# A hybrid gMLP and mLSTM decoder layer on 8 cores: the up projection moved between the head tiles, w_down kept in SBUF, the mLSTM gates computed as rows

## The reference

```python
def _layer(...):
    a = rmsnorm(h, norm_mix)
    z = a @ w_in                                     # (B, T, 3080)
    u, vg, q, k, vm, o, zi, zf = jnp.split(z, SPLITS, axis=-1)
    u = gelu(u); vg = layernorm(gelu(vg), gm_ln_g, gm_ln_b)
    y_gm = _gmlp_mix(u, vg, gm_ws, gm_bs, gm_len)    # u * (tril(W_s) v + b), per chunk
    ig = zi + ml_b_i; lf = log_sigmoid(zf + ml_b_f)
    hm, state = _mlstm(q, k, vm, ig, lf, state, ml_len)
    y_ml = sigmoid(o) * rmsnorm(hm per head)
    h = h + concat([y_gm, y_ml]) @ w_out
    f = rmsnorm(h, norm_ffn) @ w_up                  # 1024 -> 4096
    h = h + square(relu(f)) @ w_down                 # 4096 -> 1024
    gate = sigmoid(rmsnorm(h, norm_ple) @ w_ple_gate)
    return h + gate * (pe @ w_ple_proj), state, vg   # then a final rmsnorm

def _mlstm_chunk(carry, inp):                        # 128 prompt tokens, or 8 of a sample
    b = cumsum(lf); g = b + m
    D = b_t - b_s + ig_s                             # masked to s <= t
    m_t = maximum(g, max_s D)
    w_intra = exp(D - m_t); w_inter = exp(g - m_t)
    s = (q k^T) * w_intra
    num = s v + w_inter * (q C); den = sum(s) + w_inter * (q n)
    h = num / maximum(abs(den), exp(-m_t))
    w_end = exp(D_last - m_last); dec = exp(g_last - m_last)
    C = dec * C + (w_end k)^T v; n = dec * n + sum(w_end k)
```

## Time and profile before

| what | us |
|---|---|
| three runs | 1131.55, 1148.24, 1186.08 |
| profiled execution | 1132.5 |
| its span on the slowest core | 1130.0 |
| spans of the eight cores | 1104.7 to 1130.0 |
| granted TensorE clock of the cores, mean | 0.931 to 0.941 |
| busy PE / DVE / ACT / POOL | 943.0 / 574.1 / 464.0 / 339.5 |

### The profile page before, as it was taken

One profiled execution on the slowest core, in us unless ns is written; L12 is line 12 of the kernel. 1 busy time (PEld: TensorE's weight loads), 2 busy tenths in 40 slices (PEclk: granted clock), 3 DMA queues, 4 the chain that ended last, 5 costly groups with the idle time before them and its releaser, 6 DMA issues.

```text
span 1129.9 us, 17655 instructions; the slowest of 8 cores (1104.7 to 1130.0 us)
## 1 busy us (share of the span) xinstructions
PE 943.0 (83%) x5508; PEld 499.0 (44%) x5508; DVE 574.1 (51%) x1424; ACT 464.0 (41%) x992; POOL 339.5 (30%) x519
## 2 busy tenths in 40 slices
PE   0179877798889978597879998999899999999965
PEld 0034444444444444254435553555355445547622
DVE  0126677658787687774203641563066227416513
ACT  0227656585655755244303531442153224305312
POOL 4125553535454554432200221212111212112100
PEclk9989887898989989789989998999999999999997
DMA  9996001522111101999999369937972993399381
GB/s 167 191 156 85 14 35 57 93 39 76 39 38 57 57 17 41 181 169 137 207 167 142 89 137 202 143 107 157 169 146 85 171 183 109 93 169 176 81 137 48
DMA packets 109149, 128.98 MB, mean 114 GB/s; under 512 B 14594, under 2 KB 91522, under 8 KB 109058
## 3 DMA queue, kind: packets, MB, share of 16 engines
q0 software_dynamic: 74416, 72.96, 45.0%
q1 hardware_dynamic: 34642, 54.90, 16.0%
HBM read 177.97 MB, written 22.84 MB: 178 GB/s over the span
## 4 chain that ended last, share of the span: by engine, by line
PE 65%; DMA 17%; DVE 7%; issue 5%; ACT 2%; SPq 2%; POOL 1%; another core or an unknown queue 0%; DVEq 0%; POOLq 0%; ACTq 0%
PE pb L192 62%; DMA AR<-w_down 11%; DVE AR L454 4%; PE pb L199 3%; DMA AR<-snT 3%; DVE AR L464 2%; ACT AR L434 2%; SPq L341 2%; DMA AR<-hscr 2%; DMA AR<-sC 1%; POOL AR L454 1%; DVE AR L471 0%; DMA AR<-xp 0%; ACT L434 0%
## 5 line engine op out<-in xcount | busy, mean ns | idle before, releaser
L192 PE MATMUL pb<-AR 128*128 128x512 bf16 (+4 forms) x4786 | 901.0, 347 | 97.6 <-DMA AR<-w_down 32.4
L192 PEld LDWEIGHTS pb<-AR 128*128 128x128 bf16 x4786 | 451.4, 102 | 514.9 <-issue 166.9
L434 ACT ACTIVATE AR<-pb 128x384 f32<-128x384 f32 (+4 forms) x379 | 192.7, 523 | 325.6 <-PE pb L192 211.9
L434 ACT ACTIVATE AR<-AR 128x128 f32<-128x128 f32 (+2 forms) x357 | 189.6, 554 | 244.2 <-DVE AR L454 117.5
L454 DVE TENSOR_TENSOR AR<-AR 128x4 f32<-128x4 f32 (+5 forms) x521 | 194.7, 391 | 178.0 <-ACT AR L434 153.4
L454 POOL TENSOR_TENSOR AR<-AR 128x1 f32<-128x1 f32 (+5 forms) x203 | 216.5, 1071 | 123.3 <-DVE AR L454 45.6
L199 PE MATMUL pb<-AR 128*128 128x128 bf16 x722 | 70.2, 233 | 80.4 <-DVE AR L454 44.2
L460 POOL TENSOR_SCALAR AR<-AR 128x1 f32<-128x1 f32 (+1 forms) x102 | 22.8, 223 | 369.9 <-ACT AR L434 306.6
L454 DVE TENSOR_TENSOR AR<-pb,AR 128x1024 bf16<-128x1024 bf16 (+2 forms) x102 | 96.6, 953 | 57.4 <-PE pb L199 47.9
L454 DVE TENSOR_TENSOR AR<-AR,pb 128x512 f32<-128x512 f32 x68 | 46.7, 686 | 145.6 <-PE pb L192 132.3
L199 PEld LDWEIGHTS pb<-AR 128*128 128x128 bf16 x722 | 53.0, 104 | 106.6 <-issue 95.5
(11 more groups left out here) (21 smaller groups left out, 96.6 us busy)
## 6 DMA issues: line engine op xcount, KB each, us to landing
AR<-w_down POOLq DMA_DIRECT2D x48, 1024.0 KB, 17.8
AR<-hscr SPq DMA_DIRECT2D x31, 512.0 KB, 8.2
hscr<-AR SPq DMA_DIRECT2D x17, 512.0 KB, 2.9
AR<-xp SPq DMA_DIRECT2D x16, 512.0 KB, 3.4
AR<-w_up POOLq DMA_DIRECT2D x4, 2048.0 KB, 34.7
y_p<-AR SPq DMA_DIRECT2D x16, 512.0 KB, 2.8
AR<-w_in POOLq DMA_DIRECT2D x6, 1024.0 KB, 54.0
AR<-sC SPq DMA_DIRECT2D x16, 256.0 KB, 4.3
```

Source lines behind the costliest of these rows:

```text
L192: ins = e.matmul(out, l, r, start=(start and i == 0), stop=(stop and i == n - 1))
L434: return S.op("act", lambda e: e.activation(out=out, in_=in_, func=func, **kw), aps(in_, bias, scale), aps(out, accum), cost, TABLES.get(f ...
```

## The change

Four things are done together.

1. **Order of the stages.** The up projection leaves the second pass. After the third tile of a group has its head done, `stage_B` (the RMSNorm before the MLP, straight from `H1`) is complete for the group, and eight pieces of `stage_up` (4 groups of 8 matmuls of 384 columns each) are due one after another between the stages of the next three head tiles. Their results go through `GS` to a new DRAM scratch `gscr` (17 x 1 MB of bf16) and come back in the second half, tile by tile.
2. **Weights.** `w_up` is loaded anew for every group but the last, as 8 pieces of 1 MB into a ring of 4 (`load_wu`): 40 loads. `w_down` is loaded once, as 8 pieces which stay: 8 loads in place of 48. `stage_down` now works tile by tile with 32 matmuls in one run into one bank.
3. **Gates.** `stage_G` computes the gates with the 4 heads on partitions and 128 tokens along the row: 16 matmuls that give 4x128, two `tensor_tensor_scan`, and some operations on 4x128; five small f32 matmuls put them back on partitions, and the mask and the maximum are summed by 4 bf16 and 4 f32 matmuls of 128 columns. `bcast_rows`, the masked maximum and the two f32 matmuls of the old gates are gone.
4. **Buffers and start.** The sample tile is the first tile. `H1` has 3 buffers in place of 5, `YT` and `KTOK`/`VAUG` 2 in place of 3, `SGM` 2 in place of 4; the projections have 2 PSUM banks in place of 3, the up projection 2 in place of 4. Constants are loaded after the first matmul. Half of the squares of the up projection are on POOL. The scheduler's model of transfers differs, and every stage has a new due time (`T_TILE` 31 in place of 18).

```diff
-        TILES = [ptile(i) for i in range(4)] + [stile] + [ptile(i) for i in range(4, NPT)]
+        TILES = [stile] + [ptile(i) for i in range(NPT)]
...
-        T_TILE = 18.0
-        T_B = T_A + T_TILE * 17 + 30.0
-        T_GRP = 98.0
+        T_TILE = 31.0
+        T_C = T_A + T_TILE * 17 + 65.0
+        T_CT = 19.0
...
-        bP = Banks([1, 2, 3])
-        bP1 = Banks([4])
-        bM1 = Banks([5, 6])
-        bM2 = Banks([7])
+        bP = Banks([1, 2])
+        bP1 = Banks([3])
+        bM1 = Banks([4, 5])
+        bT = Banks([0])
+        bUp = Banks([6, 7])
...
+        def stage_G(t):
...
+            for k in range(2):
+                S.mm(pz[0:4, k * 128:(k + 1) * 128],
+                     [(WIN[:, kc, 3072 + 4 * k:3076 + 4 * k], at[:, kc, :]) for kc in range(8)])
+            act(L1, pz[0:4, 128:256], AF.Exp, bias=NBF[0:4, :], scale=-1.0)
+            act(L1, L1, AF.Ln, bias=1.0)
+            scan(BP, one if ty == 0 else CR[0:4, CR_FIRST:CR_FIRST + 128], L1, 0.0, ALU.mult, ALU.add)
+            stt("dve", AA, pz[0:4, 0:128], GB[0:4, 0:1], BP, ALU.add, ALU.add)
+            if ty == 0:
+                scan(MX, AA, AA, MRUN[0:4, :], ALU.max, ALU.max)
...
+            pm = PB[bM1.next()][:, :].rearrange("p (h t) -> p h t", h=4)
+            for h in range(4):
+                S.mm(pm[:, h, :], [(IDB, MTB[ty]), (CR[0:4, CR_EH + h * 128:CR_EH + (h + 1) * 128], MX)])
+            for h in range(4):
+                act(BIG1[:, h, :], pm[:, h, :], AF.Exp, bias=gc[:, h:h + 1], scale=-1.0)
...
+        def load_wu(k, c):
+            if k == len(GROUPS) - 1:
+                return
...
+            load_cast(buf, w_up_v[:, :, c * 512:(c + 1) * 512])
+
+        def stage_up(k, c):
...
+            for f in range(4):
+                ps = PB[bUp.next()][:, 0:n]
+                S.mm(ps, [(wu[:, kc, f * 128:(f + 1) * 128], A2T[k % 2][:, kc, 0:n]) for kc in range(8)])
+                out = gs[:, 0:nt, f, :]
+                rl = RL[f % 2][:, 0:n]
+                act(rl, ps, AF.Relu)
+                v = rl.rearrange("p (j t) -> p j t", t=128)
+                tt("dve" if f % 2 == 0 else "pool", out, v, v, ALU.mult)
+            for j, t in enumerate(grp):
+                S.dma(t["gs"][:, c * 512:(c + 1) * 512], gs[:, j, :, :].rearrange("p f t -> p (f t)"))
...
+        def load_tile(t):
             g = t["g"]
...
+            t["h2"] = H2[g % 4]
+            S.dma(G[g % 3], t["gs"].rearrange("p (f t) -> p f t", f=32))
+            S.dma(t["h2"], t["hs"])
+
+        def stage_down(t, nn):
+            gt = G[t["g"] % 3]
+            ps = PB[bD.next()][:, :]
+            for c in range(4):
+                S.mm(ps, [(gt[:, c * 8 + f, :], WD[nn][c][:, f, :]) for f in range(8)],
+                     start=(c == 0), stop=(c == 3))
```

More of the change, by code:

```diff
@@ L169, in _record @@
         o.preds = self._link(o, reads, writes)
+        for a_ in after:
+            o.preds[a_.idx] = True
         o.tok = None
@@ L174, in op, with dma @@
         return self._record("op", eng, fn, None, None, cost, reads, writes, table)
-    def dma(self, out, in_, eng="sp", **kw):
+    def dma(self, out, in_, eng="sp", after=(), **kw):
         nb = 1
@@ L180, in dma @@
         nb *= max(_dsize(in_.dtype), _dsize(out.dtype))
[L181 removed]
+        return self._record("dma", eng, out, in_, kw, 0.95 if eng == "pool" else 0.08, [in_], [out], None, nb, after)
     def mm(self, out, pairs, start=True, stop=True):
@@ new lines, in build @@
+        events.append((T_A - 13.0, setup2, ()))
+        for t in TILES:
+            T0 = T_A + T_TILE * t["g"]
+            for st_, off in ((stage_N, -14.0), (stage_P, 0.0), (stage_G, 8.0), (stage_P1, 13.0), (stage_M1, 24.0), (stage_M2, 45.0),
+                             (stage_B, 58.0)):
+                events.append((T0 + off, st_, (t,)))
+        T_U = 0.0
+        for k, grp in enumerate(GROUPS):
+            T_U = max(T_U, T_A + T_TILE * grp[-1]["g"] + 60.0)
+            step = len(grp) * T_TILE / 8.0
+            if k >= len(GROUPS) - 2:
+                step = 8.0 if k == len(GROUPS) - 2 else 3.5
+            for c in range(8):
+                lead = 34.0 if k < len(GROUPS) - 1 else 0.0
+                tl = T_U + c * step - lead
+                if k == len(GROUPS) - 2 and c >= 4:
+                    tl = max(tl, T_A + T_TILE * 16 + 9.0)
+                events.append((tl, load_wu, (k, c)))
+                events.append((T_U + c * step, stage_up, (k, c)))
+            T_U += 8 * step
@@ new lines, in build, with load_wd, load_second @@
+        bD = Banks([6, 7, 1, 2])
+        bC0 = Banks([0])
+        bC1 = Banks([3, 4])
+        bSt = Banks([5])
+        def load_wd(nn, c):
+            load_cast(WD[nn][c], w_down[c * 1024:(c + 1) * 1024, nn * 512:(nn + 1) * 512]
+                      .rearrange("(f p) n -> p f n", p=128))
+        def load_second():
+            for c in range(2, 4):
+                load_wd(0, c)
+            for c in range(4):
+                load_wd(1, c)
+            load_cast(WP, w_pp.rearrange("(k p) n -> p k n", p=128))
+            load_cast(WG, w_pg.rearrange("(k p) n -> p k n", p=128))
```

506 lines of the change are left out of this document (239 added, 267 removed).

## The result

The changed kernel took 1172.46 us (median of 4 runs, 1164.44 to 1175.89) against 1141.19 us for the kernel before on the same chip. The ratio is 1.034, with a 95% interval of 1.024 to 1.044: **slower**. Executions in which the cores of one die ran slower, at a lower granted clock, stand in no ratio; here that leaves a median of 1134.14 us for the kernel before. I had forecast 1112 us (1060 to 1165), with 0.45 on faster. Both the value and the likeliest sign were wrong. The profiled execution of the changed kernel took 1175.9 us.

What follows compares the result with a forecast made beforehand. The prediction took PE, busy 83% of the span, as the bound, with most to win in the head pass. Its stages 187 + 539 + 367 + 17 gave 1110 us, with 2.5 outside the span 1112 us; range 1060 to 1165.

Steps and rivals of the forecast that it cites:

- Start: From the kernel's start until the first group's up projection can begin: 187 us, with the last `sC` there at about 115.
- the 71 us: From the last `sC` landing to the first up matmul: 61 us of PE work, taken as 71, between 61 and 78.
- Steady stage: Up groups between head tiles, until two of eight pieces of the last group are done: 539 us.
- work term, 502: PE's counted work while up groups run between head tiles: 502 us.
- loss term, 37 us: PE's lost time over 13.3 head tiles, half the old head pass's loss, 2.8 us a tile: 37 us, ends 7 and 75.
- Rest and tail: After two pieces of the last up group: 367 us for PE's remaining work and waits, plus 17 us at the end.
- transfer wait: After the last tile's projection, PE waiting for the remaining weights until `w_pg` is needed: 12 us (0 to 30).
- My estimate of 95 us for 13.5 MB: Transfer time for the weights left after the last tile's projection, against about 87 us of PE work until `w_pg`.
- Costed at nothing: Work on ScalarE (24 us in a tile of 40), VectorE (17 of 40), POOL and scratch transfers, taken as covered.
- ScalarE's rival: Up matmuls wait for banks ScalarE must empty, 0.4 us at each of 181 groups: +73, 1185 us; chance 0.16.
- The loads' rival: The burst of loads moves with `w_up`, 8 us a group for 5 groups: +40, 1152 us; chance 0.14.
- The wholly filled case: Up projection fills the head pass wholly, loss 0.5 us a tile, start 180, transfer wait 5: 1068 us; chance 0.22.

Runs made afterwards that it cites:

- e_csb: Changed kernel with the four `sC` loads given a buffer each and issued ahead of `w_out`; ratio 1.0197 to the kernel before.
- e_nh5: Changed kernel with five `H1` buffers in place of three, one early `w_down` piece loading in the transition instead; 1143.28 us, ratio 1.0112 to the kernel before.
- e_onp: Changed kernel with `o_Np` stored from a copy, late in the second half; 1142.89 us, ratio 1.014 to the kernel before.
- b_gates: Kernel before with the row gates alone, its order, rings and up projection kept; ratio 1.0351 to the kernel before.
- b_gsplit: Kernel before with the row gates alone, their f32 matmuls of 128 columns each split into two bf16 ones; ratio 1.0185 to the kernel before.
- a_oldgates: Changed kernel with the gates of the kernel before; ratio 1.0548 to the kernel before.
- a_oldall: `e_all` with the gates of the kernel before, which have no f32 split; 1137.37 us, ratio 1.0052 to the kernel before.
- e_all: Changed kernel with late `o_Np` copy, four early `sC` buffers, f32 matmuls split into bf16, four `H1` and three `gscr` staging buffers; 1096.70 us, ratio 0.9711.

## Why the prediction was wrong

**Start (187, measured 208).** The first half was right: the last `sC` that holds PE landed at 116.3 (forecast 115) and PE then had 43.5 us of busy time at a clock of 0.80, some 35 of work. The term that failed is the 71 us from there to the first up matmul. It took 91, of which PE was busy 75.7, for the 61 us of work (in it 12 f32 matmuls of 128 columns, at this clock 9.2 us in place of 3). So of the 20 us that it took beyond 71, 6 are the f32 matmuls, and idle time and clock are the rest. The granted clock was 0.79 there, so PE spent a good part of it at 1.2 GHz, after 116 us in which it had been busy 43.5 and a last wait of 20 us for `sC`. I priced this stretch between the pace of the old head pass (clock 0.88) and no loss. I had no term for a colder clock, and should have taken the upper end, 78 us, at least. The wait for `sC` is not shown to be its cause: `e_csb`, without that wait, begins at 197, but from 112 to 160 us its clock is 0.75, hardly above the 0.71 of the changed kernel.

**Steady stage (539, measured 583).** Its work term, 502, was too small by 13.3 x 4 x 0.23 = 12 us: the f32 matmuls cost 0.48 us in this stage, outside my bounds of 0.083 and 0.33. I scaled a bf16 row by the ratio of two tiny matmuls, of 4 and 8 columns. The loss term, 37 us, came out at 583 - 514 = 69 by my count of the work, and at 76 us of idle time by the trace, which has 507 us busy there. It was inside my ends (7 to 75), but for a reason that the text doesn't have. I reasoned about gate latency covered by up work. What there was is (a) 35 us of idle PE by 690, nearly all from three `H1` buffers behind `hscr` and `xp` transfers (`e_nh5`), and (b) 41 us of 100 idle from 690 to 790, with `o_Np` and the `gscr` stores on the chain (`e_onp`). Both are buffers that come free by a transfer that lands late. For `o_Np` the full DMA engines are shown as the reason, by the 1.3 us in `e_onp`; for `hscr`, `xp` and `gscr` I infer it. I had counted the transfers as time to be had (73% of the engines needed) and not as a latency that each buffer adds.

**Rest and tail (384, measured 384).** Right, and so was what it rests on: resident `w_down` removes the waits of the earlier trace rows, and 330.5 of 349.5 us are PE's. PE is idle 19 us of these, 17.4 of them from 790.5 to 830 us, where the DMA share is still 1.06: this is the transfer wait, for which I had 12 (0 to 30). But the larger part of it, the 41 us idle from 690 to 790, falls inside the steady stage, where my sum had no transfer wait. My estimate of 95 us for 13.5 MB left out the 10.8 MB of SP's queue.

**Costed at nothing.** VectorE was busy 20.6 us in a tile of 44 in the steady stage, where I had 17 of 40, ScalarE 21 where I had 24. What I didn't see is that the price of the row gates hangs on the order: in the old one they cost PE more than they save (`b_gates`, `b_gsplit`), in the new they are worth 1.5 to 3.4% (`a_oldgates`, `a_oldall`).

**The rivals.** ScalarE's rival (1185, chance 0.16) came nearest in time and was wrong in its mechanism. Its trace sign is PE idle before the 128x384 matmuls; that is 5.3 us. Its 181 groups were also miscounted: up to two pieces of the last group there are 168. The waits on ScalarE from 224 to 690 stand mostly before other matmuls and come from x. The loads' rival did not happen as such: no wait on `w_up` stands among PE's largest. The wholly filled case (1068) is where the kernel goes once the buffers are there: it gave the steady stage 509 us, and `e_all` has 508. It missed the start (180 against 198) and the rest.

**The case that I lacked** is the one on the slow side: a buffer that comes free by a transfer. The rows for it were there. In the earlier trace rows, from 505 to 584, a stretch with the DMA share at 1.05 had PE busy 60.5 of 79 us. The change makes three rings smaller (`H1` 5 to 3, heads' tiles 3 to 2) and adds 136 stores behind which squares wait. One line of the form "buffers x tile time, less the landing under load" would have asked the question. With three buffers of 44 us each (583 / 13.3), what the path of a tile from x to the store leaves of 132 us is the slack for two transfers.

What stays open: what the store and the loads of the transition cost each without the other; what each of the five edits of `e_all` is worth there, besides the split; and why the clock up to 112 us is 0.76 to 0.88 on the cores of the changed kernel (0.82 in `e_csb`, 0.77 in `e_all`, without the wait on `sC`) against 0.93 to 0.98 before.

## What to carry to other kernels

When work is moved into a stage, list the rings that become smaller and what frees each slot. A slot that a transfer frees costs the landing time under load, not the median one. Look also at what a late small store reads, since a load that overlays it stands at the head of an in-order queue. A saving on an engine has a price only in an order: the row gates with the split cost 1.9% in the old order and save 3.4% in the repaired new one, so price such an edit after the order is fixed, and repair the waits before deciding on the work.

## What the runs showed of the hardware

- An f32 matmul of 4x128 by 128 columns leaves two records and takes 0.48 us at a clock of 0.96 (23.2 us for 48), 0.53 over the whole kernel (36.3 for 68). Two bf16 ones in its place take 0.28 at a clock of 1.00 (13.5 us for 96 in `e_all`), and each of those 0.14, above the 0.083 of a 128x128 one in the earlier trace rows.
- A store of 512 separate f32 numbers landed after 23.2 us while the loads filled the engines (share 1.06), 22.0 to 28.3 on the eight cores. Issued where the share was 0.12, its packets were done after 1.3 us.
- With POOL's squares of 128x384 (0.845 us) gone, several VectorE operations with two SBUF inputs became shorter (128x4 from 0.546 to 0.374 us), and those with one PSUM input stayed (128x129 at 0.341 and 0.343).
- A store of 128 KB to DRAM has a median landing of 8.0 us, and single ones on the chain took 20 to 22 us, while the cast loads of the other queue take 79.2% of the engines.
